# The last expert's block of a top-2 mixture of experts, taken through the table of added blocks

## What is computed

```
grp  = argmax(lg)                          # one of 4 groups
top_v, top_i = lax.top_k(le_g, TOP_K)      # 2 of the 8 experts in it
eid  = grp[:, None] * EXPERTS_PER_GROUP + top_i
...
for e in range(N_EXPERTS):                 # 32
    h = jax.nn.silu(x2d @ moe_w_gate[e]) * (x2d @ moe_w_up[e])
    y = y + combine[:, e:e + 1] * (h @ moe_w_down[e])
```

## Time and profile before

| | us |
|---|---|
| three runs | 1187.73, 1181.83, 1187.94 (median 1187.73) |
| the profiled execution | 1185.88 |
| its span, first to last instruction | 1184.1 |
| PE busy | 1077.9 (91%) |
| PEld / DVE / ACT / POOL busy | 826.7 / 489.2 / 286.4 / 197.3 |
| mean granted PE clock | 0.976 of full |
| read from HBM | 173.24 MB |

### The profile page before, as it was taken

The page is one execution under the profiler, slowest core; times in us unless marked ns, Lnnn a source line. Parts: engine busy times, 40 slices in busy tenths (PEclk is TensorE's granted clock), DMA queues, the critical chain, the costliest instruction groups (busy, mean ns, idle before and its releaser), DMA issues. The chain is left out here.

```text
span 1184.1 us, 25171 instructions
## 1 busy us (share of the span) xinstructions
PE 1077.9 (91%) x10717; PEld 826.7 (70%) x10717; DVE 489.2 (41%) x1154; ACT 286.4 (24%) x571; POOL 197.3 (17%) x211
## 2 busy tenths in 40 slices
PE   5999999599988999999999999999995999986874
PEld 5888888487877887888777888886453555553541
DVE  4455555655555644555547201001454422211126
ACT  3233233345544441000153210000111111101102
POOL 4000000143454400000000049000001222211120
PEclk9999999899999999999999999999996999999997
DMA  8042221200000003229312222910977899999975
GB/s 242 4 108 56 56 67 46 61 19 4 4 4 4 4 12 89 72 71 212 96 55 69 57 83 57 258 46 18 406 288 273 315 416 415 414 417 416 417 316 217
DMA packets 114050, 183.08 MB, mean 155 GB/s; under 512 B 10370, under 2 KB 88734, under 8 KB 105243
## 3 DMA queue, kind: packets, MB, share of 16 engines
q1 hardware_dynamic: 107293, 168.59, 41.0%
q0 software_dynamic: 5168, 8.56, 2.0%
q10 hardware_dynamic: 1485, 4.39, 1.0%
HBM read 173.24 MB, written 17.55 MB: 161 GB/s over the span
## 5 line engine op out<-in xcount | busy, mean ns | idle before, releaser
L180 PE MATMUL rk_ps<-xT,rk_w 128*128 128x260 f32 x768 | 172.6, 385 | 0.0
L180 PEld LDWEIGHTS rk_ps<-xT,rk_w 128*128 128x128 f32 x768 | 144.6, 190 | 26.9 <-issue 2.7
L180 PE MATMUL psv<-xT,w_merge 128*128 128x260 f32 x480 | 107.7, 383 | 0.0
L180 PEld LDWEIGHTS psv<-xT,w_merge 128*128 128x128 f32 x480 | 91.1, 190 | 13.9
L2123 DVE SCALAR_TENSOR_TENSOR ex_sg<-tl_psA,ex_slot_rs,ex_sg 128x128 f32<-128x128 f32 x32 | 11.2, 351 | 139.9 <-ACT ex_sg L1923 139.7
L180 PE MATMUL uv_psu<-xT,w_uv 128*128 128x260 f32 x256 | 57.5, 383 | 1.2 <-ACTq L1066 1.2
L180 PE MATMUL mg_psp<-ya,w_merge 128*128 128x260 f32 x256 | 57.6, 383 | 0.0
L180 PE MATMUL psv<-xT,w_uv 128*128 128x260 f32 x256 | 57.4, 382 | 0.0
L180 PE MATMUL mg_psp<-r_all,w_merge 128*128 128x260 f32 x256 | 57.4, 382 | 0.0
L699 PE MATMUL ck_b<-ck_X,ck_V 64*64 64x64 f32 x1280 | 52.6, 223 | 4.0 <-issue 3.3
L1396 POOL TENSOR_TENSOR spare<-spare,sv 128x4096 f32<-128x4096 f32 x1 | 8.8, 8850 | 277.8 <-DVE r_all L1365 277.8
(11 more groups left out here) (485 smaller groups left out, 1992.3 us busy)
## 6 DMA issues: line engine op xcount, KB each, us to landing
wd<-in_moe_w_down SPq DMA_DIRECT2D x15, 1024.0 KB
rk_w<-in_w_in SPq DMA_DIRECT2D x24, 512.0 KB, 6.1
tl_x<-in_moe_w_down SPq DMA_DIRECT2D x9, 1024.0 KB
w_uv<-in_w_in SPq DMA_DIRECT2D x16, 512.0 KB, 5.3
w_merge<-in_w_in SPq DMA_DIRECT2D x16, 512.0 KB, 4.1
xT<-in_moe_w_gate SPq DMA_DIRECT2D x5, 1024.0 KB, 20.0
xT<-in_moe_w_up SPq DMA_DIRECT2D x5, 1024.0 KB, 23.6
bonus_all<-in_moe_w_gate SPq DMA_DIRECT2D x5, 1024.0 KB
```

Of the source, the lines that this page charges most:

```text
L180: last = eng.matmul(out[:, h, 0:TH], weights[:, k, :], xT[:, k, h * TH:(h + 1) * TH], start=(k == 0), stop=(k == NK - 1))
```

## The change

The last expert's first block is no longer written out. `NB` = 31 blocks are written out, the table has 17 entries, and `extra` of the last expert is at least 1, so its block is a table entry like the added ones. Since the table is in the order of the experts, its entry is the last one; the number of passes is one more than the number of blocks beyond an expert's first. The ranks of expert 31's pairs get 64 added, so that they fall into table entries. The passes use the second buffer of each pair (`psg`, `sg`, `hT`, `psd`, `yo`) in place of the first.

```
-EXTRA = 2 * T // CAP
+NB = NE - 1
+EXTRA = 2 * T // CAP + 1
...
-            for k in range(SLOTS, NE):
+            for k in range(SLOTS, NB):
...
-            eng.wait_ge(s_y[0], n * 16 + NE // 2 * 16)
-            eng.wait_ge(s_y[1], NE // 2 * 16)
+            eng.wait_ge(s_y[0], NE // 2 * 16)
+            eng.wait_ge(s_y[1], n * 16 + (NE // 2 - 1) * 16)
...
-            scatter_block(NE - 1)
...
-            for k in range(NE):
+            for k in range(NB):
...
-            down_block(NE - 1)
+            down_block(NB - 1)
...
-                eng.wait_ge(s_h, q + NE)
-                gate_up(SPARE, 0, halves_of[0], 0)
+                eng.wait_ge(s_h, q + NB)
+                gate_up(SPARE, 0, halves_of[0], 1)
...
                 do(eng.tensor_scalar(extra[:, :], need[:, :], -1.0, 0.0, ALU.add, ALU.max))
+                do(eng.tensor_scalar(extra[:, NB:NE], need[:, NB:NE], 1.0, None, ALU.max))
...
-                do(eng.tensor_copy(rki[:, :, :], rk[:, :, :]))
+                do(eng.scalar_tensor_tensor(out=rki[:, :, :], in0=oh[:, :, :, NB:NE].rearrange("p c t e -> p c (t e)"),
+                                            scalar=float(CAP), in1=rk[:, :, :], op0=ALU.mult, op1=ALU.add))
...
-            result_block(NE - 1)
+            result_block(NB - 1)
```

More of the change, by code:

```diff
@@ L1488, in phase_tail @@
         mine = sg[:, :, :].rearrange("p n s -> p (n s)")[:, 0:6 * NE].rearrange("p (t c e) -> p t c e", c=2, e=NE)
-        to_slot, to_x = x2s[:, 0:2 * NTT * CAP], x2s[:, 2 * NTT * CAP:2 * NTT * (CAP + NE)]
+        to_slot, to_x = x2s[:, 0:2 * NTT * CAP], x2s[:, 2 * NTT * CAP:2 * NTT * (CAP + 2 * EXTRA)]
         at_slot = to_slot.rearrange("p (t c s) -> p t c s", c=2, s=CAP)
@@ L1493, in phase_tail @@
         at_slot_x = to_slot.rearrange("p (c t s) -> p c t s", c=2, s=CAP)
-        work = to_x.rearrange("p (c t e) -> p c t e", c=2, e=NE)
+        work = to_x[:, 0:2 * NTT * NE].rearrange("p (c t e) -> p c t e", c=2, e=NE)
         at_list_x = to_x.rearrange("p (c t q) -> p c t q", c=2, q=2 * EXTRA)
@@ L1649, in _ @@
                 eng.wait_ge(s_now, q * 2 + 2)
-                eng.wait_ge(s_yo, q + (NE + 1))
+                eng.wait_ge(s_yo, q + (NB + 1))
                 eng.sem_inc(s_gate, 1)
-                scatter(0, sidx_now[:, 0:1])
+                scatter(1, sidx_now[:, 0:1])
             eng.wait_ge(s_in[0], n * 16 + (NE // 4 + 1) * 16)
@@ L1839, in _ @@
                 eng.wait_ge(m.s_gate_up[SPARE], q * 32 + 160)
-                eng.wait_ge(s_h, q + NE)
-                gate_up(SPARE, 0, halves_of[0], 0)
[L1842 to L1845, removed]
+                eng.wait_ge(s_h, q + NB)
+                gate_up(SPARE, 0, halves_of[0], 1)
+                eng.wait_ge(s_h, q + (NB + 1))
+                eng.wait_ge(s_hte, q + NB)
+                turn_h(1)
+                eng.wait_ge(s_hte, q + (NB + 1))
                 eng.wait_ge(m.s_down[SPARE], q * 16 + 80)
-                eng.wait_ge(s_yo, q + NE)
-                down(SPARE, 0)
+                eng.wait_ge(s_yo, q + NB)
+                down(SPARE, 1)
                 eng.wait_ge(s_in[0], q * 16 + (NE // 4 + 2) * 16)
@@ L1944, in _ @@
                 eng.wait_ge(s_now, q * 2 + 1)
-                eng.wait_ge(s_gu, q + (NE + 1))
-                silu(0, rs_now[:, 0:1])
+                eng.wait_ge(s_gu, q + (NB + 1))
+                silu(1, rs_now[:, 0:1])
                 eng.sem_inc(s_gu_free, 1)
-                eng.wait_ge(s_ht, q + (NE + 1))
-                hidden(0)
+                eng.wait_ge(s_ht, q + (NB + 1))
+                hidden(1)
                 eng.wait_ge(s_t, q + (NE // 2 + 2))
@@ L2220, in _ @@
                 eng.wait_ge(s_now, q * 2 + 1)
[L2221 to L2224, removed]
+                eng.wait_ge(s_sg, q + (NB + 1))
+                product(1, rs_now[:, 0:1])
+                eng.wait_ge(s_down, q + (NB + 1))
+                eng.wait_ge(s_y[1], q * 16 + (NE // 2 - 1) * 16)
                 eng.tensor_copy(sidx_now[:, :], sidx[:, bass.ds(q + NE, 1)]).then_inc(s_now, 1)
-                result(0)
+                result(1)
                 eng.sem_inc(s_d_free, 1)
```

## The result

Over six runs each the kernel after has a median of 1196.24 us (1191.59 to 1199.74), the kernel before 1186.34 us (1181.83 to 1187.94). The ratio is **1.0097, 95% interval 1.0069 to 1.0125**: 8 to 15 us slower. The forecast was 1194.9 us, slower, by a second pass that starts late. The profiled execution took 1195.99 us, with a span of 1193.9 us.

The account below looks back on a forecast made before the run. Weight loads bound the blocks, then the unoverlapped end chain. The second gate_up at 1149.35 + 1.7 clock + 11.52 + 0.3 scatter puts the results' read at 1162.9, +7.2 us: 1193.1 profiled, 1194.9 against the median; range 1189.5 to 1200.

Parts of the forecast that it names:

- The old pass had work, and there are two passes now: Expert 17's 69 pairs leave five rows for the old pass; after, 31 written-out blocks and two passes, no weights saved.
- Rival (c): The old pass was empty, so one pass remains and a block goes: chain 7.6 us sooner, 1180.1 us; chance 0.05.
- The weights' chain: Second pass's loads wait for the first's silu, issued 1141.85, in 7.5 us later at 1149.35, when its gate_up begins.
- The rows' chain: Second pass's gather, issued 1141.48, lands 5.8 us later; turned and copied by 1149.1, or 1151.2 if it takes 7.9.
- The clock in the pass: PE's idle before the second gate_up lowers the clock to 0.50, costing 1.7 us; the other end is 0.
- An unchanged final part: Behind the read of the results, the final part was to stay as before; the read itself comes 5 to 9 us later.
- rival (a): The clock stays up in the second pass and the rest holds: +5.5 us, 1193.2 us; chance 0.27.
- The residual reads: Moved behind the second pass's down load, done by 1158.3, ahead of the results' read at 1162.9: no cost, 4.6 us spare.
- rival (b): Residual reads drain slowly, so the second pass's scatter lands late, plus a branch cost: +10 to +10.6 us, about 1198; chance 0.14.
- The table's vector work: Routing's one added instruction and 17 entries instead of 16: below 0.4 us in all, hidden behind a down.
- the way round the loop: Engines branching back for the second pass: 0 to 1.3 us, taken as 0; 0.4 us more on PE at the high end.
- Rival (d): Second pass's weights and rows are in when the first's down ends at 1144.9: gate_up starts there, 1188.4 us; chance 0.07.

Follow-up runs that it names:

- f4: Kernel after with a table where only expert 31 has an entry, expert 17's five extra pairs put into its block, so one pass; ratio 0.9957 to before.
- e1: Kernel after with its two passes written out one after the other in place of the loops; ratio 1.0059 to before.
- f1: Kernel after with 26 identity transposes on PE behind each pass's down; ratio 1.0091 to before.
- f2: Kernel after with 40 identity transposes on PE between the residual rows' matmuls and the wait for the results; ratio 1.0083 to before.
- f3: Kernel after with 26 identity transposes behind each pass's down and 16 ahead of the final sum; ratio 1.0099 to before.
- g2: Kernel after with 44 identity transposes on PE behind each pass's down and 7 more behind the turn; ratio 1.0067 to before.
- e4: Kernel after's table, but its first entry (expert 17) written out as block 31 and the loop running over the rest (expert 31); ratio 1.0006 to before.
- g1: Kernel after with one more semaphore, so that SP's loads of a pass wait for POOL's gather; the intended order wasn't reached; ratio 1.0098 to before.
- e2: As e1, with a weight slot of its own for each pass (3 and 5); ratio 1.0081 to before.
- e3: As e2, with the second pass's rows gathered together with the first's, so that no pass gathers or turns; ratio 1.0027 to before.
- g3: e3 with 40 identity transposes on PE ahead of the final sum; ratio 0.9992 to before.
- g4: g3 with the two passes on two buffers and their scatters' rows read straight from the table; ratio 1.0014 to before.

## Why the prediction was right

**The old pass had work, and there are two passes now**: right; two pairs of loads into slot 5, and after's gather of expert 31's rows in the software queue's bytes. Rival (c), an empty old pass, fell; f4 prices it at 5.1 us in place of 7.6.

**The start of the first pass**: forecast 9.13 us after the start of block 30's `gate_up` (1128.42 to 1137.55), measured 9.13 (1125.60 to 1134.73, the end of `down`).

**The weights' chain**: 8.1 us from the end of one `gate_up` to the start of the next, right in sum, as e1 shows it alone (8.1). Its two parts were off by 0.4 us each, in opposite directions, and that they cancel is luck: the loads were issued 0.2 us after the end of `gate_up` where the forecast had 0.6 (it waited for the end of `silu`, and SP went 0.2 us after its start), and they took 7.9 us where it had 7.5.

**The rows' chain**: the term that was mis-sized. The gather was taken at 5.8 us and measured 7.2, the turn ran at half the clock (2.0 in place of 1.1), and so the rows ended the wait, 2.5 us later than the sum had it: a gap of 10.6 us, outside the 7 to 9 that the prediction gave as its sign. Its upper bound, 7.9, was reached or passed in f1, f2, f3 and g2 (7.9 to 8.6). The 5.44 us that it took for the low end were a poor guide, since that gather moved no rows. The old kernel made one pass, so table entry 1, gathered in it, was empty. The windows of before just ahead of its landing (1153.57) show what was left of the residual reads, and then nothing:

```profile
1152.50:1153.00 0.50, 0.00 (x0) 0.00 (x0) 0.02 (x1) 0.00 (x0) 0.00 (x0) 1.00 0.08 25
1153.00:1153.50 0.50, 0.00 (x0) 0.00 (x0) 0.00 (x0) 0.00 (x0) 0.10 (x1) 1.00 0.00 0
```

**The clock in the pass**: right in kind and low in size, 2.8 us (6.5 against 3.7) in place of 1.7, the price seen in the earlier trace rows. In half-microsecond windows of after the clock is at 0.50 from 1144.2 to 1154.5, so all but the last 0.8 us of the second `gate_up` lie in this dip; in the earlier trace rows it fell 0.4 us after the `gate_up` had begun and was back at 1100.3. Why this dip was longer stays open. That PE's idle brings it is shown by g2, where it is filled and the `gate_up` takes 3.7 us; the seven other profiles with two passes and a wait have 5.1 to 6.5. But idle doesn't always do it: 2.2 us ahead of block 30's `gate_up` left it at 3.7 us in before, e1, e4, f1 and f2 and made it 5.4 in g1 and g2.

**"An unchanged final part" was wrong.** F grew by 2.3 us. The step that failed took the old final part as fixed: before, PE was at the slow clock from 1154.9 to 1158.4, under work that nothing waits for, and was up again when the sum began. After, residual matmuls end at 1163.4, PE stands for 6 us, and the dip falls on the sum. f2 takes it away. The 14 profiles agree: with 2.9 to 6.0 us of idle just ahead of the sum (after, e1, e2, e3, f1, f4, g1) its first matmuls took 5.4 to 6.7 us and F was 29.4 to 30.7; with 0.2 to 1.9 us (before, e4, f2, f3, g2, g3, g4) they took 3.7 us and F was 28.2 to 28.4.

**Hidden terms and rivals**: rival (a), the clock stays up, fell, since the clock was down in the pass and in the sum. The residual reads were done by 1156, 7 us ahead of the read, so rival (b) fell as a mechanism, though P alone grew by 10.4 us, about its 10 to 10.6, for other reasons. The table's vector work cost nothing that e4 shows, and the way round the loop nothing that after's timeline shows on DVE. The Trainium skill ("Runtime: NRT & Kernel Launch", "Instruction fetch mechanics") names a stall at a taken branch whose target is not among the fetched instructions. The trace of after shows none: DVE's first instruction of the second pass starts at 1148.47, before the last of the first pass ends at 1148.55. Rival (d) would need the lead: e3 is that kernel.

**The sum.** P + F grew by 12.6 us against a forecast of 7.2: rows 2.5, clock in the pass 1.1, final part 2.3 make 5.9 on top of 7.2, or 13.1; the other half a microsecond came out less in the small terms (silu to the issue of the read took 7.95 us where the sum had 8.1, and the first pass's `gate_up` 3.5 us where it had 3.7). The ratio stands for 11.5 us (8 to 15), the two medians of six runs are 9.9 us apart; 12.6 lies within what the ratio allows. The sum was thus short by a third or more, and that 1194.9 came within 1.3 us of the median, 1196.24, is partly luck: the forecast stood on a median of 1187.73 for the kernel before, and over six runs that was 1186.34, 1.4 us less. One sum in the prediction was off as well: with the gather at 5.44, the weights 0.5 us sooner and the clock kept, its own terms give +4.9 us, not +4.7.

What stays open: whether a gather issued well ahead of the loads is fast in the looped kernel too. In the six profiles in which it came 0.02 us ahead to 0.26 us behind them (with 0.44 us to the second load), it took 7.2 to 8.6 us; in the one in which it was 0.98 us ahead (e1) it took at most 4.2. But e1 has no loops, and g1 missed its order, so order and loops aren't told apart.

## What to carry to other kernels

Before moving work from written-out code to a loop with one buffer, count what that work gets besides code: its loads' lead, its gather's lead, its place behind a busy engine. A shared slot turns a prefetched load into a load in line as soon as two passes follow each other, and where two transfers are late, taking one away shows only a part of the loss; take both. And check with the data how many passes there will be: here five rows in one expert decided the sign.

## What the hardware showed beyond the forecast

- A gather of 30 rows (0.12 MB) issued within 0.3 us of 2.1e6 bytes of weights lands 7.2 to 8.6 us after its issue, and within 4.2 us in the one profile in which it was issued 0.98 us ahead of them (e1). That the order within a microsecond is what is worth the 3 us isn't shown, since e1 also has no loops.
- A semaphore raised by the instruction behind an indirect DMA on POOL let SP go 0.02 us after the start of POOL's 1 us of work for it, as the profile of g1 places that work.
- Idle on PE is paid for later and elsewhere: with the clock at 0.50 (1.2 GHz) for all or part of them, the second `gate_up` took 5.1 to 6.5 us and the final sum's first matmuls 5.4 to 6.7; at 1.00 both took 3.7 (g2), and transposes of the identity kept it there.
